# Full and half-width expert passes run side by side in a mixture-of-experts layer, and the last scatter moves ahead of a branch

## The chip, the cores and the metric

One core of one Trainium2 chip runs the whole program. The metric is device time in microseconds (us) of one execution. The kernel before has a median of 1798.19 us over 3 runs, from 1795.90 to 1801.63 us. Everything is float32 in memory.

## What is computed

Two layers of a transformer block on 256 latent and 256 context tokens of width 1024. Only the end of it matters here: in the second layer the feed-forward part is a mixture of 8 experts, and each of the 256 latent tokens goes to its two best.

```python
def swiglu(h, w1, w3, w2):
    return (jax.nn.silu(h @ w1) * (h @ w3)) @ w2

def moe_ffn(h, router, w1, w3, w2):
    ...
    logits = (ht @ router).astype(jnp.float32)
    top_v, top_i = lax.top_k(logits, TOP_K)
    wts = jax.nn.softmax(top_v, axis=-1)
    ...
    def expert_step(acc, p):
        e1, e3, e2, cw = p
        return acc + cw[:, None] * swiglu(ht, e1, e3, e2), None
```

w1 and w3 are 1024 x 2816, w2 is 2816 x 1024. After it come a norm, a gate and the residual sum. One expert's weights are 33 units of 1 MB: 22 for w1 and w3 ("up"), 11 for w2 ("down").

## The kernel before, in words

**Passes.** Each expert is one pass p. The expert order is found on the chip from the token counts: pass 0 is fixed, then the experts follow from the fullest to the emptiest. A pass collects ("gathers") the tokens of its expert into slots by matmuls with a selection matrix (`gather`, then `turn_selection`, which transposes that matrix for later), runs 11 chunks (FC = 11, numbered c) of 256 columns of the inner width, and puts the results back to their tokens by matmuls with the turned selection (`scatter`, four pieces), which VectorE adds to `y_moe` (`added`). Passes 0 to 4 have 128 slots; pass 1 has 32 more in a side computation (WIDE, its tiles end in `_wide`); passes 5, 6 and 7 have 64 slots ("narrow", `NARROW = range(5, 8)`). After these eight come up to three further passes for experts with more tokens than slots, each behind a branch on a number computed on the chip (`extra`); in the profiled execution none is taken.

**Full passes.** A product of float32 operands is made of three matmuls of rounded parts. So each 1 MB weight unit is split: ScalarE writes the rounded high part (`high`, L1360) and VectorE the rest (`low`, L2018), into a ring of `W_RING` = 4 places. The raw units arrive by DMA in a ring of `RAW_RING` = 5 places; a raw place is free for the next load once its unit is split. `unit_ready` on TensorE waits for the split.

**Narrow passes.** They take the raw unit as it is, in one float32 product on 64 columns of the array, so there is no split, but a raw place is free only when TensorE has used it.

**The steps.** `run_steps` gives, for step i, what TensorE does in a row: the up matmuls of chunk i (`up_chunk`, two units), the transposes of chunk i-1's activations (`turn_chunk`, into PSUM bank 2), the down matmuls of chunk i-2 (`down_chunk`, one unit); behind it, at certain chunks, a scatter piece of the pass before (chunks 3 to 6) or the gather for the next (chunk 7). Between them ScalarE makes silu (`silu`, L1434), VectorE the product (`product`, L2067), ScalarE copies the turned columns (`columns_turned`, L1445, for narrow chunks L1442) and VectorE makes their low part (L2078). The order on each engine is the order of the code in that engine's `run`; every engine waits on semaphores and works strictly in its own order.

**Where the splits stand.** In `run` on ScalarE and VectorE the place of each split is fixed by `split_behind`: at the step that uses split unit s, the unit s + 4 is split. So the splits run up to a ring ahead of their use. `output` copies a finished pass from PSUM for its scatter; `half_high`/`half_low` and `columns_high`/`columns_low` copy the gathered tokens from PSUM.

**The end.** On TensorE the last pass's four scatters (`finish`) stand in the Else part of the branch on further passes.

Of the kernel before, what the change touches and what calls it, by code (L numbers as in the profile page):

```python
# [32 lines left out]
P = 128  # L33
# [259 lines left out]
EXTRA = (2 * LAT - 1) // (P + 1)  # L293
PASSES_OF = EXPERTS + EXTRA
# [4 lines left out]
def run_steps(passes):  # L299

    g0, g1 = passes[0] * FC, (passes[-1] + 1) * FC
    for g in range(g0, g1 + 2):
        yield g if g < g1 else None, g - 1 if g0 <= g - 1 < g1 else None, g - 2 if g0 <= g - 2 else None


def pass_units():

    out = []
    for passes in RUNS:
        for up, _, down in run_steps(passes):  # L310
            out += [("up", up, 0), ("up", up, 1)] if up is not None else []
            out += [("down", down)] if down is not None else []
    assert len(out) == PASSES_OF * EXPERT_UNITS
    return out
# [3 lines left out]
UNIT_AT = {key: m for m, key in enumerate(UNIT_LIST)}  # L318
RUN_END = tuple((passes[-1] + 1) * EXPERT_UNITS for passes in RUNS)


def run_last(r):
    return (RUNS[r][-1] + 1) * FC - 1
# [12 lines left out]
NARROW, SLOTS = range(5, EXPERTS), 64  # L336
HALF_GROUPS = P // SLOTS


def is_narrow(p):  # L340

    return p in NARROW
# [10 lines left out]


SPLIT_LIST = [m for m, key in enumerate(UNIT_LIST) if not is_narrow(unit_of_expert(key)[0])]
SPLIT_OF = {m: s for s, m in enumerate(SPLIT_LIST)}

# [6 lines left out]
def split_limit(r):  # L364

    return split_end(r) + (0 if is_narrow(RUNS[r][-1]) else W_RING - 1)


def split_behind(r, key):

    s = SPLIT_OF[UNIT_AT[key]] + W_RING
    return [s] if s < split_limit(r) else []
# [192 lines left out]
TURN_BANK, SCATTER_BANK = 2, 3  # L565
# [3 lines left out]
def build(nc, ctx, units, x_in, ctx_in, const_in, cols_in, wsm_in, gw2_in, lam_in, rope_in, out):  # L569
# [85 lines left out]
    picked = at("picked", A_GL + 2952, [P, 2, 3, EXPERTS])  # L655
    order, order_parts = at("order", A_AM + 320, [P, EXPERTS, EXPERTS]), at("order_parts", A_GL + 3888, [P, 3, EXPERTS, EXPERTS])
    xt_plain = at("xt_plain", A_ACTT, [P, 2, KT, P])
    selT_plain = at("selT_plain", A_GL + 1280, [P, 2, 2, P])
    eT_plain = at("eT_plain", A_GL + 1792, [P, 2, 256])
    ey_plain = at("ey_plain", A_OD, [P, 512])  # L660
# [133 lines left out]
    def down_bank(p, h):  # L794

        return 4 + 2 * (p % 2) + h

    def up_bank(g):

        return 0 if g // FC == WIDE else (g + WIDE * FC) % 2  # L800

    def gather_bank(p, n):

        return SCATTER_BANK if p == WIDE + 1 else down_bank(p, n)
# [5 lines left out]
    def select_place(p):  # L810
        return sel if p < EXPERTS else sel_more[p - EXPERTS]
# [101 lines left out]
    def _(pool):  # L913
# [18 lines left out]
        def select_narrow(p):  # L932

            twice = const[:, C_IOTA:C_IOTA + SLOTS].unsqueeze(1).to_broadcast([P, HALF_GROUPS, SLOTS])
            for tt in range(2):
                pool.tensor_scalar(sel[:, tt, :].rearrange("p (j n) -> p j n", j=HALF_GROUPS), twice, route[:, tt, 4, p:p + 1],
                                   route[:, tt, 3, p:p + 1], ALU.is_equal, ALU.mult).then_inc(esem("sel"), 1)
# [11 lines left out]
        for p in range(1, EXPERTS):  # L949

            pool.wait_ge(esem("selT"), p)
# [15 lines left out]
    def _(act):  # L967
# [399 lines left out]
        def half_high(p, n):  # L1367
            act.wait_ge(esem("gathered"), 2 * p + n + 1)
            if is_narrow(p):
                act.activation(xt_plain[:, p % 2, 4 * n:4 * n + 4, 0:SLOTS],  # L1370
                               psum[:, gather_bank(p, n), 0:4 * SLOTS].rearrange("p (k n) -> p k n", n=SLOTS),
                               ACT.Copy).then_inc(esem("xt_hi"), 1)
                return
            act.activation(xt_hi[:, p % 2, 4 * n:4 * n + 4, :],
                           psum[:, gather_bank(p, n), :].rearrange("p (k n) -> p k n", n=P),
                           ACT.Copy).then_inc(esem("xt_hi"), 1)

        def selection_turned(p):
            act.wait_ge(esem("selT"), p + 1)
            if p >= 2:  # L1380
# [1717 lines left out]
```

## Time and profile before

| | before |
|---|---|
| median of 3 runs | 1798.19 us |
| profiled execution, time | 1800.37 us |
| profiled execution, span | 1798.4 us |
| TensorE busy | 1694.8 us (94%) |
| VectorE busy | 1015.4 us (56%) |
| ScalarE busy | 794.1 us (44%) |
| mean granted TensorE clock | 0.973 of full speed |
| moved by DMA | 407.53 MB, mean 227 GB/s |

The expert layer is the second half: pass 0 begins near 973 us after the span's start, pass 2 near 1217 us, the narrow passes near 1520 us, and the last down matmul ends near 1778 us. In the rows below times are us from the span's start. PE is TensorE, DVE VectorE, ACT ScalarE, POOL GpSimd, SP SyncE. "[2.0 <-X]" says that the engine sat idle for 2.0 us and that X ended it. Matmuls overlap, so the distance of two starts is what one costs, and its own length is longer. PEclk is the granted TensorE clock as a share of 2.4 GHz.

### The profile page before, as it was taken

To read this page: it belongs to the slowest core of one execution; us is meant where nothing else is said; L and a number is where in the kernel's file an instruction comes from. 1 tells how busy PE (TensorE), PEld (TensorE's weight loads), DVE (VectorE), ACT (ScalarE), POOL (GpSimd) and SP (SyncE) were. 2 spreads that over 40 slices of the span, in tenths; PEclk is the share of its full clock that TensorE was granted. 3 is DMA by queue.
4 is the path that set the end of the run, shared out by engine and by line. 5 is a ranking of instruction groups with operands and counts; after the bars stand their busy time and mean duration, and the time that the engine had idled before them with its cause. 6 is when DMAs were issued, how large, how long until landed. Compare 5 with 4: busy or idle time off the path is not lost.

```text
span 1798.4 us, 25945 instructions
## 1 busy us (share of the span) xinstructions
PE 1694.8 (94%) x10337; PEld 1310.9 (73%) x10337; DVE 1015.4 (56%) x1403; ACT 794.1 (44%) x1225; POOL 55.0 (3%) x40
## 2 busy tenths in 40 slices
PE   6999989999999999999887999999999998889886
PEld 4877668988888888887677887777788887444442
DVE  3335656677677434643766986667799895101012
ACT  4416545622212223725546765556677774100101
POOL 0000000000000000000000530000000000000000
PEclk8999989999999999999978999999999999999998
DMA  8412053244467422231024977668999897899997
GB/s 332 150 71 71 1 201 145 79 185 170 185 237 263 179 94 94 80 117 48 24 71 151 357 287 258 237 235 354 344 351 360 343 360 295 327 421 421 420 421 327
DMA packets 56830, 407.53 MB, mean 227 GB/s; under 512 B 6322, under 2 KB 6450, under 8 KB 7808
## 3 DMA queue, kind: packets, MB, share of 16 engines
q1 hardware_dynamic: 56128, 404.38, 58.6%
q8 instruction: 85, 1.39, 0.3%
q0 software_dynamic: 288, 0.79, 0.1%
q10 hardware_dynamic: 288, 0.63, 0.1%
q14 instruction: 41, 0.34, 0.1%
HBM read 404.73 MB, written 1.05 MB: 226 GB/s over the span
## 4 chain that ended last, share of the span: by engine, by line
PE 82%; DMA 7%; DVE 5%; ACT 4%; issue 2%; SPq 0%; POOL 0%; DVEq 0%; ACTq 0%
PE psum L2243 60%; PE psum L2850 4%; DMA raw_more<-units 4%; DMA raw<-units 4%; PE psum L2860 2%; PE psum L2748 2%; PE psum L2806 1%; PE psum L2876 1%; PE psum L2888 1%; PE psum L2442 1%; PE psum L2269 1%; DVE w_lo L1551 1%; PE psum L2466 1%; PE psum L2538 1%; PE psum L2260 1%
## 5 line engine op out<-in xcount | busy, mean ns | idle before, releaser
L1551 DVE TENSOR_TENSOR w_lo<-raw,w_hi 128x1024 fp32r<-128x1024 f32 x130 | 153.0, 1220 | 144.9 <-ACT w_hi L980 144.6
L2243 PE MATMUL psum<-act_hi,w_hi 128*128 128x512 f32 (+1 forms) x608 | 221.1, 364 | 2.1 <-DVE w_lo L1551 2.1
L2243 PE MATMUL psum<-act_hi,w_lo 128*128 128x512 f32 (+1 forms) x608 | 218.7, 360 | 0.0
L2243 PE MATMUL psum<-act_lo,w_hi 128*128 128x512 f32 (+1 forms) x608 | 218.7, 360 | 0.0
L980 ACT ACTIVATE w_hi<-raw 128x1024 fp32r<-128x1024 f32 x130 | 130.3, 1053 | 161.8 <-DMA raw<-units 87.5
L2018 DVE TENSOR_TENSOR w_lo<-raw,w_hi 128x2048 fp32r<-128x2048 f32 x75 | 171.5, 2289 | 41.7 <-ACT w_hi L1360 41.4
L1360 ACT ACTIVATE w_hi<-raw 128x2048 fp32r<-128x2048 f32 x75 | 143.8, 1918 | 68.4 <-PE psum L2243 43.2
L2018 DVE TENSOR_TENSOR w_lo<-raw_more,w_hi 128x2048 fp32r<-128x2048 f32 x49 | 112.1, 2289 | 46.2 <-ACT w_hi L1360 46.0
L2243 PE MATMUL psum<-w_hi,act_hi 128*128 128x256 f32 (+1 forms) x368 | 130.2, 354 | 3.4 <-DVE w_lo L1551 1.7
L2243 PE MATMUL psum<-w_hi,xt_hi 128*128 128x512 f32 x332 | 132.1, 398 | 0.0
L2243 PE MATMUL psum<-w_lo,xt_hi 128*128 128x512 f32 x332 | 129.9, 391 | 0.0
L2243 PE MATMUL psum<-w_hi,xt_lo 128*128 128x512 f32 x332 | 129.7, 391 | 0.0
L2067 DVE TENSOR_TENSOR e_act<-e_sil,psum 128x256 f32<-128x256 f32 (+1 forms) x88 | 32.2, 366 | 172.4 <-ACT e_sil L1434 172.4
L2243 PEld LDWEIGHTS psum<-act_hi,w_hi 128*128 128x128 f32 x608 | 115.5, 190 | 19.1 <-DVE w_lo L1551 2.7
L2243 PEld LDWEIGHTS psum<-act_hi,w_lo 128*128 128x128 f32 x608 | 115.3, 190 | 17.6
L2243 PEld LDWEIGHTS psum<-act_lo,w_hi 128*128 128x128 f32 x608 | 115.4, 190 | 16.5
L2243 PE MATMUL psum<-w_lo,act_hi 128*128 128x256 f32 (+1 forms) x368 | 123.1, 334 | 0.0
L2243 PE MATMUL psum<-w_hi,act_lo 128*128 128x256 f32 (+1 forms) x368 | 123.0, 334 | 0.0
L1360 ACT ACTIVATE w_hi<-raw_more 128x2048 fp32r<-128x2048 f32 x49 | 94.0, 1918 | 65.7 <-DMA raw_more<-units 35.0
L1434 ACT ACTIVATE e_sil<-psum 128x256 f32<-128x256 f32 (+1 forms) x88 | 29.4, 334 | 197.5 <-PE psum L2850 193.4
L1608 DVE SCALAR_TENSOR_TENSOR folded<-raw,c_cols,folded 128x512 f32<-128x512 f32 x140 | 101.5, 750 | 3.3
L2243 PEld LDWEIGHTS psum<-w_hi,act_hi 128*128 128x128 f32 x368 | 69.8, 190 | 26.0 <-issue 12.0
(363 smaller groups left out, 3249.3 us busy)
## 6 DMA issues: line engine op xcount, KB each, us to landing
raw<-units SPq DMA_DIRECT2D x275, 1024.0 KB, 5.1
raw_more<-units SPq DMA_DIRECT2D x107, 1024.0 KB, 6.7
X<-ctx_in SPq DMA_DIRECT2D x1, 1024.0 KB, 8.5
X<-x_in SPq DMA_DIRECT2D x1, 1024.0 KB, 10.6
out<-X SPq DMA_DIRECT2D x2, 512.0 KB, 2.8
const<-const_in ACTq DMA_DIRECT2D x1, 524.0 KB, 7.4
rope<-rope_in POOLq DMA_DIRECT2D x2, 256.0 KB, 4.9
wsm<-wsm_in SPq DMA_DIRECT2D x1, 384.0 KB, 7.0
```

The costliest lines, as they stand in the source:

```text
L980: act.activation(w_hi[:, w_slot(i), part], raw[:, i % RING, part], ACT.Copy).then_inc(hi_ready, 1)
L1360: act.activation(w_place(m)[0], raw_place(m), ACT.Copy).then_inc(esem("w_high"), 1)
L1434: act.activation(e_sil[:, g % 2, 0:n], psum[:, up_bank(g), 0:n], ACT.Silu).then_inc(esem("sil"), 1)
L1551: ins = dve.tensor_tensor(w_lo[:, w_slot(i), part], raw[:, i % RING, part], w_hi[:, w_slot(i), part].bitcast(F32), ALU.subtract)
L1608: ins = dve.scalar_tensor_tensor(total, part, share, total, ALU.mult, ALU.add)
L2018: dve.tensor_tensor(lo, raw_place(m), hi.bitcast(F32), ALU.subtract).then_inc(esem("w_ready"), 1)
L2067: dve.tensor_tensor(e_act[:, g % 2, 0:n], e_sil[:, g % 2, 0:n], psum[:, up_bank(g), n:2 * n], ALU.mult).then_inc(esem("act"), 1)
L2243: ins = pe.matmul(dst, lhs(a), rhs(b), start=first and n == 0, stop=last and n == 2)
L2260: ins = pe.matmul(bank(key)[group, 0:256], c_cols[:, k, :], raw[:, n % RING, k * 256:(k + 1) * 256], start=k < 4, stop=k >= 4)
L2748: ins = pe.matmul(psum[:, gather_bank(p, n), (k % 4) * slots:(k % 4 + 1) * slots], src[:, tt, k * P:(k + 1) * P], select_place(p)[:, tt, 0 ...
L2850: ins = pe.matmul(psum[SLOTS * j:SLOTS * (j + 1), up_bank(g), 0:2 * P].rearrange("p (g n) -> p g n", g=2), xt_plain[:, p % 2, k, 0:SLOTS], ...
L2860: ins = pe.matmul(psum[SLOTS * h:SLOTS * (h + 1), down_bank(p, 0), :], eT_plain[:, g % 2, SLOTS * j:SLOTS * (j + 1)], weight[:, j * D_MODE ...
```

## The change

Three things change in the code.

1. The narrow passes become 3, 5 and 7, each beside the full pass ahead of it: the pairs are 2 and 3, 4 and 5, 6 and 7. The ranks are handed out so that the same three emptiest experts stay narrow (`PLACE_OF_RANK`). In a pair one step holds both: up of the full chunk, up of the narrow one, turn of the full one and of the narrow one, down of both. A step thus takes six units, 6 MB.
2. In the pairs the full chunks have PSUM bank 0 for up and banks 4 and 5 for down, the narrow ones banks 1 and 6; both kinds turn into bank 2. Tiles of the narrow passes get places of their own. Every split of a pair is written in the step that uses it (`splits_at` gives `[s]`), where before it was s + 4. The gather for the next pair is cut into pieces that stand at chunks 7, 8, 9 and 10; the scatters stand at chunks 2 to 5 (full pass, or pass 1) and 6 to 9 (narrow pass); the outputs stand at chunk 2, ahead of the splits of that step.
3. On TensorE `finish` stands ahead of the branch. Since two passes (6 and 7) are then still to be put back, it has eight scatters and not four. On ScalarE the outputs of the last passes move into the branch.

The diff, cut to its core. The order of passes, steps, splits and gather pieces:

```diff
+PLACE_OF_RANK = (0, 1, 2, 5, 3, 6, 4, 7)
...
-NARROW, SLOTS = range(5, EXPERTS), 64
+NARROW, SLOTS = (3, 5, 7), 64
+FIRST_PAIR = 2
...
+def run_steps(r):
+
+    rows = []
+    for p in RUNS[r]:
+        if not is_narrow(p):
+            beside = (p + 1,) if is_narrow(p + 1) else ()
+            rows += [tuple(q * FC + c for q in (p,) + beside) for c in range(FC)]
+    for i in range(len(rows) + 2):
+        yield tuple(rows[j] if 0 <= j < len(rows) else () for j in (i, i - 1, i - 2))
...
-def split_behind(r, key):
-
-    s = SPLIT_OF[UNIT_AT[key]] + W_RING
-    return [s] if s < split_limit(r) else []
+def splits_at(r, key):
+
+    s = SPLIT_OF[UNIT_AT[key]]
+    if r == 0 and s >= SINGLE_SPLITS:
+        return [s]
+    return [s + W_RING] if s + W_RING < (split_limit(r) if r else SINGLE_SPLITS) else []
...
+def gather_pieces(r, p, c):
+
+    if r or p == 0 or is_narrow(p) or not 0 <= c - GATHER_STEP < 4:
+        return []
+    a = p + 1 if p == WIDE else p + 2
+    pieces = [[(a, 0)], [(a, 1)], [(a, 2), (a + 1, 0)], [(a + 1, 1), (a + 1, 2)]][c - GATHER_STEP]
+    return [piece for piece in pieces if piece[0] <= EXPERTS]
```

ScalarE's `run`, as it is now (VectorE's has the same order, with `low`, `product` and `half_low`):

```diff
+            for ups, turned, downs in run_steps(r):
+                full = [g for g in ups if not is_narrow(g // FC)]
+                for g in full:
+                    p, c = divmod(g, FC)
...
+                    if p >= FIRST_PAIR:
+                        for q in outputs_at(r, p, c):
+                            output(q)
+                    for s in splits_at(r, ("up", g, 0)):
+                        high(s)
...
+                    for s in splits_at(r, ("up", g, 1)):
+                        high(s)
+                    if p != WIDE:
+                        silu(g)
+                if len(ups) == 2:
+                    for g in downs[:1]:
+                        for s in splits_at(r, ("down", g)):
                             high(s)
+                    silu(ups[1])
+                for g in turned:
+                    columns_turned(g)
...
+                for g in full:
+                    p, c = divmod(g, FC)
+                    for q, piece in gather_pieces(r, p, c):
+                        half_high(q, piece) if piece < 2 else selection_turned(q)
```

TensorE's turn and end:

```diff
         def turn_chunk(g):
 
-            pe.wait_ge(esem("act"), g + 1)
-            if g:
-                wait_turned_columns(g - 1)
+            pe.wait_ge(esem("act"), CHUNK_AT[g] + 1)
+            for h in CHUNKS[max(CHUNK_AT[g] - 2, 0):CHUNK_AT[g]]:
+                wait_turned_columns(h)
...
         def finish(p):
-            for n in range(4):
-                scatter(p, n, n)
+            for q in last_passes(0) if p < EXPERTS else (p,):
+                for n in range(4):
+                    scatter(q, n, n)
 
         def extra(k):
+            finish(RUNS[k][-1])
             with pe.If(run_valid(pe, k)):
...
-            with pe.Else():
-                finish(EXPERTS + k - 1)
```

How the change moves instructions shows at three places.

ScalarE in a full pass before, around the gather for the next pass at chunk 7. `w_hi` is the high part of a weight unit, `xt_hi` the gathered tokens, `e_sil` silu, `eT_hi` the turned columns, `more_arrived` the semaphores of the raw ring.

```order
L1434 ACTIVATE e_sil<-psum 128x256 [waits e_act,e_w_used]
L1445 ACTIVATE eT_hi<-psum 128x256 [waits e_w_used,e_turned]
L1360 ACTIVATE w_hi_more<-raw 128x2048 [waits more_arrived1,e_w_used]
L1374 ACTIVATE xt_hi<-psum 128x512 [waits e_gathered] x2
L1383 ACTIVATE selT<-psum 128x256 [waits e_scattered,e_selT]
L1360 ACTIVATE w_hi<-raw 128x2048 [waits more_arrived2,e_w_used]
L1360 ACTIVATE w_hi<-raw_more_149 128x2048 [waits more_arrived3,e_w_used]
```

The same place now, in a pair, at chunk 7 and up to the next silu.

```order
L1560 ACTIVATE eT_hi<-psum 128x256 [waits e_w_used,e_turned]
L1558 ACTIVATE eT_plain<-psum 128x128 [waits e_w_used,e_turned]
L1488 ACTIVATE xt_hi<-psum 128x512 [waits e_gathered]
L1473 ACTIVATE w_hi<-raw 128x2048 [waits more_arrived0,e_w_used]
L1473 ACTIVATE w_hi<-raw 128x2048 [waits more_arrived1,e_w_used]
L1550 ACTIVATE e_sil<-psum 128x256 [waits e_act,e_w_used]
```

Both have a copy of gathered tokens ahead of two splits. Before, those splits are of units used a ring later; now the first `w_hi` behind the copy is that of the unit with which TensorE's next step begins.

TensorE in a pair now, from the end of a narrow up chunk to the begin of the next step's up (the 11 rows of the down matmuls between are left out by "...").

```order
L3016 MATMUL psum<-raw_more_153,xt_plain 64x256 x7
L3057 MATMUL psum<-const,e_act 128x128 [waits e_eT_hi,e_eT_lo,e_act]
L3057 MATMUL psum<-const,e_act 128x128
L3054 MATMUL psum<-const,e_act_plain 128x128 [waits e_eT_lo,e_eT_hi,e_act]
L2394 MATMUL psum<-w_hi,eT_hi 128x512 [waits e_w_ready,e_ey_lo,e_eT_lo]
...
L3026 MATMUL psum<-raw,eT_plain 64x512 [waits more_arrived0,e_ey_hi,e_eT_hi]
L3026 MATMUL psum<-raw,eT_plain 64x512 x3
L2970 MATMUL psum<-ey_hi,selT 128x512 [waits e_added,e_selT_copy,e_ey_lo]
L2970 MATMUL psum<-ey_lo,selT 128x512
L2394 MATMUL psum<-w_hi,xt_hi 128x512 [waits e_w_ready,e_act]
```

Before, one turn stood in each step, and it waited for the copies of the step before. Now the narrow turn (L3054) waits for `e_eT_lo`, the low part of the full chunk that was turned in the row ahead of it.

## Rows read from the trace of the kernel before

**Rows 1.** Busy time by stretch: from:to, length, busy us (count) per engine, PEclk, DMA share, GB/s
```profile
1303.25:1336.95 33.70, 33.70 (x154) 27.73 (x152) 30.18 (x21) 25.21 (x20) 0.00 (x0) 1.00 0.88 339
...
1597.93:1634.67 36.74, 30.39 (x207) 15.29 (x206) 1.44 (x5) 3.30 (x12) 0.00 (x0) 1.00 1.01 421
1212.09:1777.90 565.81, 534.30 (x2943) 365.96 (x2939) 283.32 (x241) 239.09 (x267) 7.22 (x8) 0.99 0.93 369
1777.90:1798.40 20.50, 5.79 (x8) 1.79 (x8) 8.24 (x14) 5.50 (x14) 0.00 (x0) 0.59 0.56 229
```

**Rows 2.** Timeline of TensorE in the full passes: start, length, line, matmuls
```profile
1212.09 0.44 PE L2888 MATMUL psum<-const,e_act 128*128 128x128 f32 x2
...
1216.66 0.50 PE L2243 MATMUL psum<-w_hi,xt_hi 128*128 128x512 f32 x1
...
1253.46 1.12 PE L2806 MATMUL psum<-ey_wide,selT_wide 64*128 64x512 f32 x2
...
1303.25 0.38 PE L2888 MATMUL psum<-const,e_act 128*128 128x128 f32 x2
```

**Rows 3.** Timeline of TensorE in the narrow passes
```profile
1592.35 0.33 PE L2888 MATMUL psum<-const,e_act 128*128 128x128 f32 x1
1592.61 1.94 PE L2860 MATMUL psum<-raw_more,eT_plain 128*64 128x512 f32 x8
1594.38 3.62 PE L2850 MATMUL psum<-raw,xt_plain 128*64 128x256 f32 x32
1597.93 0.33 PE L2888 MATMUL psum<-const,e_act 128*128 128x128 f32 x1
...
1652.12 1.12 PE L2806 MATMUL psum<-ey_plain,selT_plain 64*128 64x512 f32 x2
```

**Rows 4.** Groups by form, ScalarE and VectorE, 1212 to 1778 us: busy us, mean ns
```profile
L1360 ACT ACTIVATE w_hi<-raw 128x2048 fp32r<-128x2048 f32 x44 | 84.4, 1919 | 35.9 <-PE psum L2243 33.0 <-DMA raw<-units 2.8
L1445 ACT ACTIVATE eT_hi<-psum 128x256 fp32r<-128x256 f32 x35 | 13.2, 378 | 3.1 <-PE psum L2888 3.1
L1434 ACT ACTIVATE e_sil<-psum 128x128 f32<-128x128 f32 x33 | 9.2, 278 | 193.4 <-PE psum L2850 193.4
L1374 ACT ACTIVATE xt_hi<-psum 128x512 fp32r<-128x512 f32 x6 | 3.6, 592 | 7.4 <-PE psum L2748 7.4
L1370 ACT ACTIVATE xt_plain<-psum 128x256 f32<-128x256 f32 x6 | 2.3, 381 | 12.0 <-PE psum L2748 12.0
L2018 DVE TENSOR_TENSOR w_lo<-raw,w_hi 128x2048 fp32r<-128x2048 f32 x45 | 103.0, 2288 | 18.9 <-ACT w_hi L1360 18.6
L2078 DVE TENSOR_TENSOR eT_lo<-psum,eT_hi 128x256 fp32r<-128x256 f32 x35 | 14.6, 417 | 1.1 <-ACT eT_hi L1445 1.1
L2067 DVE TENSOR_TENSOR e_act<-e_sil,psum 128x128 f32<-128x128 f32 x33 | 9.5, 287 | 172.4 <-ACT e_sil L1434 172.4
```

**Rows 5.** The chain that ended last, in order of time, 1500 us to the end
```profile
1521.73 4.69 DMA raw_more<-units
...
1584.86 3.69 PE psum L2748 x32
```

**Rows 6.** Busy time by stretch, around idle spells of TensorE: columns as in rows 1
```profile
954.50:959.10 4.60, 0.00 (x0) 0.00 (x0) 2.48 (x6) 4.16 (x12) 0.00 (x0) 0.97 0.00 0
959.10:965.70 6.60, 5.70 (x32) 4.34 (x33) 3.30 (x6) 3.28 (x8) 0.00 (x0) 0.50 0.43 159
...
1531.50:1535.70 4.20, 4.15 (x11) 3.42 (x12) 0.52 (x2) 0.38 (x1) 0.00 (x0) 0.50 0.00 0
...
1556.00:1564.00 8.00, 6.58 (x49) 3.21 (x47) 1.08 (x3) 0.53 (x2) 0.00 (x0) 1.00 1.01 423
```

**Rows 7.** Timeline of TensorE and ScalarE: idle spells inside and at the end of the narrow passes
```profile
1531.55 0.66 PE L2888 MATMUL psum<-const,e_act 128*128 128x128 f32 x2 [8.28 <-DVE eT_lo L2078]
...
1783.12 3.75 PE L2806 MATMUL psum<-ey_plain,selT_plain 64*128 64x512 f32 x6 [5.24 <-issue]
1784.04 1.28 ACT L1501 ACT_TABLE_LOAD   x1 [5.39 <-issue]
```

More of the change, by code:

```diff
@@ L296, with is_narrow @@
 RAW_RING, W_RING = 5, 4
[L299 to L303, printed above, removed]
+NARROW, SLOTS = (3, 5, 7), 64
+FIRST_PAIR = 2
+def is_narrow(p):
+    return p in NARROW
+def run_steps(r):
[6 more added lines that the diff above has]
+        yield tuple(rows[j] if 0 <= j < len(rows) else () for j in (i, i - 1, i - 2))
+CHUNKS = [g for r in range(len(RUNS)) for ups, _, _ in run_steps(r) for g in ups]
+CHUNK_AT = {g: n for n, g in enumerate(CHUNKS)}
 def pass_units():
     out = []
[L309 to L312, printed above, removed]
+    for r in range(len(RUNS)):
+        for ups, _, downs in run_steps(r):
+            out += [("up", g, i) for g in ups for i in range(2)]
+            out += [("down", g) for g in downs]
     assert len(out) == PASSES_OF * EXPERT_UNITS
@@ new lines, in run @@
+                    if p != WIDE:
+                        silu(g)
+                if len(ups) == 2:
+                    for g in downs[:1]:
+                        for s in splits_at(r, ("down", g)):
+                            high(s)
+                    silu(ups[1])
+                for g in turned:
+                    columns_turned(g)
+                if len(ups) < 2:
+                    for g in downs[:1]:
+                        for s in splits_at(r, ("down", g)):
+                            high(s)
@@ L1511, in extra @@
             with act.If(run_valid(act, k)):
+                for q in last_passes(k):
+                    output(q)
                 for s in range(split_limit(k), split_end(k) + W_RING):
@@ L2123, in _ @@
+            for q in last_passes(r):
+                output(q)
         descending_once = const[:, C_DESC:C_DESC + EXPERTS]
@@ L2933, in run @@
         def run(r):
[L2934 to L2947 removed]
+            for ups, turned, downs in run_steps(r):
+                for g in ups:
+                    up_chunk(g)
+                for g in turned:
+                    turn_chunk(g)
+                for g in downs:
+                    down_chunk(g)
+                for g in ups[:1]:
+                    p, c = divmod(g, FC)
+                    for q, n in scatters_at(r, p, c):
+                        scatter(q, n)
+                    for q, piece in gather_pieces(r, p, c):
+                        gather_piece(q, piece)
+                    if c == GATHER_STEP and (p == 0 or r and p + 1 < PASSES_OF):
                         gather(p + 1)
```

390 lines of the change are left out of this document (229 added, 161 removed).

## The prediction

> **What bounds the kernel now.** I read the busy shares by stretch first. In a full pass TensorE is busy for all of the 33.70 us of four chunks, 8.43 us a chunk, with the DMA engines at 0.88 [rows 1]. In a narrow pass DMA is at 1.01 and TensorE is busy for 30.39 of 36.74 us [rows 1] and 421 GB/s, so a unit of 1.05 MB takes 2.49 us and a chunk's three take 7.47. So full passes are bound by TensorE and narrow ones by DMA, and laying one beside the other looks like a gain: a pair's step needs six units, 14.9 us, of DMA, and TensorE needs 8.43 for the full chunk and 5.58 for a narrow one whose data is there (from turn to turn, [rows 3]), 14.0 us. Now the two take 8.43 + 7.47 = 15.9 us one after the other. The stretch that the change rewrites, from the turn at 1212.09 (pass 1, chunk 9) to the end of the last down matmul at 1777.9, is 565.8 us, of which TensorE works 534.3 [rows 1]. It holds one large wait, 8.28 us at 1531.55 [rows 7], where the kinds of pass change.
>
> Next I read what feeds TensorE. A split is 1.92 us on ScalarE and then 2.29 us on VectorE [rows 4]; before it is hidden, since splits run four units ahead. The change gives this up in the pairs: each split stands in the step that uses it, behind everything that ScalarE did in the step before.
>
> **An ordinary step of a pair**, by the chain of waits, t = 0 at TensorE's first full up matmul. The matmuls of a full chunk are 36 in 8.43 - 0.2 us [rows 1, 2], 0.228 each: up 24, to 5.5, done 5.65. ScalarE then makes silu (0.4) and splits the down unit, 6.05 to 8.0; VectorE's low part ends at 10.3. Meanwhile the narrow up, 3.6 us [rows 3], has ended at 9.1 to 9.2; its product on VectorE (0.29) waits behind the low part, to 10.55; the low part of the turned full columns (0.42) follows, to 10.95 [rows 4]. Only then may TensorE turn the narrow chunk, from 11.0 to 11.3: 1.5 us idle behind the full turn. Now two paths run to the next step: TensorE's down matmuls, 12 x 0.23 and 1.8 for the narrow one [rows 3], to 15.8; and ScalarE's copy of the narrow turn (0.28), the split's high part (1.92), VectorE's low part (2.29), with semaphores to 15.9. **Step: 15.9 us**, not 14.9, and with no reserve between the two paths. Transfers are in time: the down unit is asked for at the end of the step before and is wanted 6.0 us later; a transfer took 4.69 us [rows 5].
>
> **The sum of the stretch.**
> - 33 steps x 15.9, less 1.0 for the first, which has no narrow turn: 523.7.
> - Scatters at the end of a step: four with the wide part, 1.6 each (1.12 and two matmuls, [rows 2]), eight full at 0.45, eight narrow at 1.1 [rows 3], less 0.1 of reserve: 17.
> - Gathers of passes 4, 6 and 8, 3.7 each as now [rows 5], and of 5 and 7, the same, with the turned selections: 19.5.
> - **Waits for a split behind a gather piece.** ScalarE reaches its copy of the gathered tokens and waits there until TensorE has ended downs, scatter and piece. Then copy 0.6, high 1.92, low 2.29, with semaphores 4.9 us [rows 4], in which TensorE has nothing to do, since the next up unit isn't split. Narrow pieces have two copies of 0.38, 5.1 us. Pieces stand at chunks 7 to 10 of pairs 1 and 2, at 7 to 9 of pair 3: 6 x 4.9 + 4 x 5.1 + 4.7 = 54.5. One more at pass 1's chunk 10, as the first pair's units are no longer split ahead: 5.1.
> - **Waits for a split behind the outputs** at chunk 2: the copy of the pass that has just ended (0.7) comes ahead of the split, 5.1 us, and 6.0 in the first pair, where `ey_wide` and both halves come first: 16.2.
> - From the turn at 1212.09 to the first pair: 4.6 as now [rows 2], and 2.0 of gather. At the end two steps with downs alone, the first again behind its split: 15.1.
>
> Together 523.7 + 17 + 19.5 + 54.5 + 5.1 + 16.2 + 6.6 + 15.1 = 657.7, against 565.8: **+92**. The wait of 8.28 us that goes is inside this difference. Ahead of the stretch, the narrow pass's first piece at pass 1's chunk 9 adds 1.9, and eight memsets in a row on VectorE in pass 0 add 2 (not shown; nothing if TensorE never waits there, 4 if each costs a round through its semaphore; the middle, since VectorE has under 1 us of reserve per chunk): +4.
>
> **The clock.** There are then 15 waits of about 5 us. Around an idle 4.60 us the granted clock fell to 0.50 for the 6.60 us behind it, and behind the 8.28 us it was 0.50 for another 4.2 [rows 6, 7]. The work done at half speed cost half of those stretches, 3.3 and 2.1 us. In the stretch with narrow waits of up to 1.4 us it stayed at 1.00 [rows 6], so I charge nothing for the 1.5 us inside each ordinary step. I take 2.5 us a wait, between those two and nearer to the second, since that one lies in expert passes as these will: 15 x 2.5 = +37. Bounds: nothing (the clock holds) and 3.3.
>
> The Trainium skill, TensorE: Matmul & The Clock Gate, section on HAM oscillation, tells of a kernel in which each tile's wait for data threw the engine back to the lower clock, so that every tile paid anew. By that rule all 15 waits pay, as summed here. No row yet shows a wait of 5 us with dense matmuls on both sides; if the clock holds there, the sum is 37 us less (rival 2).
>
> **The end.** Now 5.24 us pass between ScalarE's last copies and TensorE's scatter, ended by no other engine [rows 7], and 20.5 us between the last matmul and the end [rows 1]. With the scatters ahead of its branch TensorE doesn't wait there itself, but VectorE's branch still stands between its last output and its adds, and there are eight adds of 0.75 us in place of four. What leaves, about 4, is taken by the four further adds, 3: -1, with -5 (all branches hidden) and +3 (none) as bounds.
>
> **Sum:** +92 + 4 + 37 - 1 = +132 on the profiled 1800.4, 1932. The median of the runs is 2.2 below the profiled time, so I forecast **1930 us**.
>
> **Rivals.**
> 1. *The splits are hidden and the pairs overlap as they are meant to*: faster. Then a step costs the larger of 14.9 and TensorE's work: 14.9 for chunks 0 to 6, 16 to 17 where a gather piece stands, near 170 us a pair, 510 in all, with 17 at both ends 527, so 39 less; with +4 and -1 that is 1800.4 - 36 - 2 = 1762. For it speaks DMA's 1.01 beside an unsaturated TensorE [rows 1]. Against it is the order: ScalarE's `w_hi` for the next step stands behind a copy that waits for that step's end. It decides where TensorE waits under 0.3 us at a step's begin; the halfway point is waits of some 2 us. 7 in 100.
> 2. *The waits are as summed, but the clock holds at full speed*: 1930 - 37 = 1893. The gaps stand 16 to 20 us apart with dense work between, unlike the one at 954 us. 13 in 100.
> 3. *More than summed*: the clock costs 3.3 us a wait (+12), or the down unit comes late, since two narrow units are on their way ahead of it; each us over its 6.0 adds one to the 18 ordinary steps, so 1 to 2.4 us late is +18 to +43. 1942 to 1985, about 1965. 17 in 100.
> 4. *It does nothing that can be measured*, waits and gains cancel: 2 in 100. It would need waits of 1.5 us where I find 5.
>
> The forecast's own case has 61 in 100, from 1905 to 1950. **Range** 1885 to 1975: it takes in rival 2 and most of rival 3, and leaves out rival 1. A measurement of this kernel tells about 0.3% (5 us) from no change. Faster 0.07, same 0.02, slower 0.91.
>
> **What would show it.** The timeline of ScalarE at chunks 7 to 10 of a pair: `xt_hi` or `xt_plain` released by a gather matmul, `w_hi` right behind it, `w_lo` on VectorE, and TensorE's next matmul released by `w_lo` after 4.9 to 5.1 us; 12 such waits, and 3 behind `ey_plain` or `ey_hi`. Ordinary steps of 15.9 us with the narrow turn released by `eT_lo` after some 1.5 us. The granted clock at 0.50 behind each long wait. DMA busy near 0.75 over the stretch, from 0.93, so that it is the bound no longer. TensorE waits for no transfer. I am wrong if steps with a gather piece are under 20 us (expected 22 to 24), if ordinary ones are near 15 or over 17, or if TensorE's waits name a DMA.

## The result, and the profile after

The change takes **1938.82 us** (median of 4 runs, 1933.78 to 1941.59), the kernel before 1799.91 in the same comparison (4 runs, 1795.9 to 1807.18): ratio 1.0755, 95% interval 1.0718 to 1.0793. The forecast was 1930 us, range 1885 to 1975. The profiled execution of the change took 1933.78 us. Each ratio below is to the kernel before in the same comparison; its median moved from 1798.5 to 1804.8 us between comparisons, so times from different ones compare to some 5 us.

The page of the changed kernel: the span, the busy times, the granted clock, and the chain that ended last.

```profile
span 1931.9 us, 25970 instructions
...
PE 1737.2 (90%) x10337; PEld 1325.1 (69%) x10337; DVE 1018.0 (53%) x1416; ACT 792.0 (41%) x1225; POOL 51.7 (3%) x40
...
PEclk8999899999999999997989999999888998899988
...
PE 71%; DVE 12%; ACT 8%; issue 7%; DMA 1%; SPq 0%; POOL 0%; DVEq 0%; ACTq 0%
```

The last row is the chain. VectorE and ScalarE hold 20% of it, and DMA 1%: what is waited for is computed, not loaded. The digits of PEclk are 8 in seven of the last fourteen slices, those of the pairs.

Busy time by stretch, columns as in [rows 1]: the rewritten stretch from the turn of pass 1, chunk 9 to the end of the last down matmul, the tail, an ordinary step (turn to turn), a step with a full scatter (up to up), a step with a gather piece, and a long wait with what follows it.

```profile
1212.25:1913.65 701.40, 576.34 (x2920) 378.37 (x2916) 285.01 (x237) 242.03 (x270) 4.69 (x6) 0.92 0.79 301
1913.65:1931.90 18.25, 6.14 (x18) 2.99 (x16) 10.79 (x18) 4.02 (x12) 0.00 (x0) 0.67 0.41 166
...
1459.51:1475.44 15.93, 14.68 (x81) 9.63 (x80) 7.74 (x7) 6.72 (x7) 0.00 (x0) 1.00 0.98 391
1509.67:1526.66 16.99, 15.47 (x81) 9.92 (x82) 8.48 (x7) 6.72 (x7) 0.00 (x0) 1.00 0.96 369
1386.27:1410.43 24.16, 18.01 (x95) 12.54 (x96) 8.43 (x7) 7.31 (x8) 0.00 (x0) 0.86 0.66 260
...
1368.75:1373.65 4.90, 0.00 (x1) 0.03 (x1) 3.13 (x3) 4.19 (x3) 0.00 (x0) 0.67 0.64 241
1373.65:1378.00 4.35, 4.35 (x12) 3.44 (x13) 2.06 (x1) 0.00 (x0) 0.00 (x0) 0.59 0.73 266
```

Against [rows 1] the stretch is 135.6 us longer (701.4 for 565.8) and the tail 2.2 shorter (18.3 for 20.5). Of the 135.6, busy TensorE time is 42 us (576.3 for 534.3), most of it the same matmuls at the lower clock, and the rest is idle time. The DMA share fell from 0.93 to 0.79.

TensorE's waits over 1190 to 1960 us: total, times, longest.

```profile
PE psum L2394 <- DVE w_lo L2144: 63.2, 22, 5.9
PE psum L3054 <- DVE eT_lo L2207: 41.0, 33, 1.3
PE psum L2394 <- DVE w_lo_more L2144: 20.7, 8, 5.0
PE psum L2970 <- DVE y_moe L2184: 2.8, 1, 2.8
```

No transfer is among them. The first and third row hold 15 waits of 4.7 to 5.9 us at the begin of a step, one more of 4.6 in the drain, and small ones. One of the 15, on all engines (start, length, engine, line; in brackets the idle time and what ended it):

```profile
1593.96 0.28 PE L2899 MATMUL psum<-sel,h_lo 128*128 128x128 f32 x1
1594.27 0.60 ACT L1488 ACTIVATE xt_hi<-psum 128x512 fp32r<-128x512 f32 x1 [7.41 <-PE psum L2899]
1594.76 3.70 ACT L1473 ACTIVATE w_hi<-raw 128x2048 fp32r<-128x2048 f32 x2
1594.90 0.69 DVE L2154 TENSOR_TENSOR xt_lo<-psum,xt_hi 128x512 fp32r<-128x512 f32 x1 [8.80 <-ACT xt_hi L1488]
1596.70 2.29 DVE L2144 TENSOR_TENSOR w_lo<-raw,w_hi 128x2048 fp32r<-128x2048 f32 x1 [1.11 <-ACT w_hi L1473]
...
1599.13 0.76 PE L2394 MATMUL psum<-w_hi,xt_hi 128*128 128x512 f32 x1 [4.90 <-DVE w_lo L2144]
```

ScalarE was idle for 7.41 us though the raw unit was there (over 1190 to 1960 us it waits for one only twice, 2.6 us in all): it stood at the copy of the gathered tokens, which could only begin when TensorE had ended its step. Only then came the split for TensorE's next matmul. The wait is copy, high part, low part, in a row, and TensorE works in none of it.

### The profile page after: what moved, and what is told of

The parts are those of the page before. It is cut to its first block, busy times and chain, and to the rows that moved or that the text cites. A ratio compares the mean times of both kernels' runs of the same rounds, so it can differ in the third digit from the quotient of the medians.

```text
span 1931.9 us, 25970 instructions
## 1 busy us (share of the span) xinstructions
PE 1737.2 (90%) x10337; PEld 1325.1 (69%) x10337; DVE 1018.0 (53%) x1416; ACT 792.0 (41%) x1225; POOL 51.7 (3%) x40
## 3 DMA queue, kind: packets, MB, share of 16 engines
HBM read 404.73 MB, written 1.05 MB: 210 GB/s over the span
## 4 chain that ended last, share of the span: by engine, by line
PE 71%; DVE 12%; ACT 8%; issue 7%; DMA 1%; SPq 0%; POOL 0%; DVEq 0%; ACTq 0%
PE psum L2394 53%; DVE w_lo L2144 4%; ACT w_hi L1473 4%; PE psum L3026 3%; PE psum L2899 2%; DVE w_lo_more L2144 1%; PE psum L2970 1%; DMA raw<-units 1%; ACT w_hi_more L1473 1%; PE psum L3042 1%; PE psum L2593 1%; PE psum L2420 1%; DVE w_lo L1677 1%; PE psum L2617 1%; PE psum L2689 1%
## 5 line engine op out<-in xcount | busy, mean ns | idle before, releaser
L2394 PE MATMUL psum<-w_hi,xt_hi 128*128 128x512 f32 x332 | 146.5, 441 | 63.5 <-DVE w_lo L2144 63.4
L2394 PE MATMUL psum<-w_lo,xt_hi 128*128 128x512 f32 x332 | 140.9, 424 | 0.0
L2394 PE MATMUL psum<-w_hi,xt_lo 128*128 128x512 f32 x332 | 138.6, 418 | 0.0
L1550 ACT ACTIVATE e_sil<-psum 128x256 f32<-128x256 f32 x55 | 20.9, 379 | 274.9 <-PE psum L2394 274.9
L2394 PEld LDWEIGHTS psum<-w_hi,xt_hi 128*128 128x128 f32 x332 | 69.4, 209 | 91.7 <-issue 69.1
L2394 PEld LDWEIGHTS psum<-act_lo,w_hi 128*128 128x128 f32 x608 | 115.6, 190 | 16.5
L2196 DVE TENSOR_TENSOR e_act<-e_sil,psum 128x256 f32<-128x256 f32 x55 | 23.0, 418 | 163.8 <-ACT e_sil L1550 163.8
```

The lines of the kernel that those rows point to most:

```text
L1550: act.activation(e_sil[:, parity(g), :], psum[:, up_bank(g), 0:256], ACT.Silu).then_inc(esem("sil"), 1)
L2196: dve.tensor_tensor(e_act[:, parity(g), :], e_sil[:, parity(g), :], psum[:, up_bank(g), 256:512], ALU.mult).then_inc(esem("act"), 1)
L2394: ins = pe.matmul(dst, lhs(a), rhs(b), start=first and n == 0, stop=last and n == 2)
```

## The experiments

**1 to 4: each suspected cost alone.** e1_splits_ahead, in `run` on ScalarE (on VectorE the same with `low`); `ahead_of` gives the up units of the next step if that is a pair's:

```diff
+                for key in ahead_of(r, i):
+                    for s in splits_at(r, key):
+                        high(s)
                 for g in full:
                     p, c = divmod(g, FC)
                     for q, piece in gather_pieces(r, p, c):
```

(and the two `splits_at(r, ("up", g, k))` of a pair's own step are gone).

> ACT and DVE split both up units of the next pair step right after the turned copies, ahead of the gather copies and the outputs; TensorE's order is that of the change. Theory A (the 15 waits of 4.7 to 5.9 us end with DVE's split only because it stands behind the gather copies or outputs on ACT and DVE): the waits go (15 x 5.0 = 75 us), with them the time at half clock behind them (34 us in the trace of the change) and some 0.7 us in each of 12 scatter steps (8 us); 1939 - 117 = about 1822 us, granted clock of the stretch back to 0.97 or more. Theory B (the stretch is held by transfers, and the splits only end a wait that a transfer would end as late): the waits on DVE are replaced by waits on DMA at the same places, and the time falls by under 40 us, to 1900 or more.

Measured: **1835.66 us**, ratio to before 1.0199 (1.0143 to 1.0254); 103 us less than the change. Its waits of TensorE:

```profile
PE psum L3067 <- DVE eT_lo L2217: 48.7, 33, 3.0
PE psum L2407 <- DVE w_lo_more L2154: 5.0, 2, 4.6
...
PE psum L2407 <- DVE w_lo L2154: 1.2, 2, 0.8
```

The waits for `w_lo` fell from 83.9 to 6.2 us; the 4.6 left is the drain's. Theory A stands: TensorE waits for no transfer in their place, and ScalarE's waits for raw units are 19.3 us in all. The missing 14 us against 1822: the narrow turn now waits up to 3.0 us in steps that hold a copy or an output too (48.7 for 41.0), with the clock at 0.66 to 0.72 for 5 us behind the three of 2.8 us and more and at 1.00 behind the next one down, 2.45 us, and the profiled stretch is 597.9 us, 103.5 less and not 117:

```profile
1212.10:1810.00 597.90, 542.96 (x2920) 359.04 (x2916) 284.53 (x237) 243.96 (x270) 5.25 (x6) 0.99 0.91 353
```

The clock, 0.92 in this stretch of the change, is 0.99 again.

e2_full_first changes TensorE's `run` alone, in steps with two up chunks:

```diff
-                for g in turned:
+                for g in turned[:1] if len(ups) == 2 else turned:
                     turn_chunk(g)
-                for g in downs:
+                for g in downs[:1] if len(ups) == 2 else downs:
+                    down_chunk(g)
+                for g in turned[1:] if len(ups) == 2 else ():
+                    turn_chunk(g)
+                for g in downs[1:] if len(ups) == 2 else ():
                     down_chunk(g)
```

> TensorE alone has another order: turn full, down full, turn narrow, down narrow, so that the narrow turn's silu has a down chunk of time to end. The narrow turn waits 1.25 us for eT_lo in each of 33 steps of the change. Theory A (in such a step the splits of ACT and DVE, which stand behind the narrow turned copies, come due next): the 1.25 us is gained, but the narrow turn is later by the full down chunk (3.6 us), the turned copies and splits behind it are later by as much, and the next up units wait; about 2 us more an ordinary step and 1 a scatter step: 1939 + 15 to 50 = 1955 to 1990 us. Theory B (the wait for the silu is just time lost): 33 x 1.25 = 41 us less, 1898 us.

Measured: **1963.77 us**, 1.0910 (1.0851 to 1.0969). Theory A. The 41 us at the narrow turn went, and the waits for `w_lo` rose from 83.9 to 135.9 us:

```profile
PE psum L2394 <- DVE w_lo L2144: 103.5, 50, 6.0
PE psum L2394 <- DVE w_lo_more L2144: 32.4, 17, 5.0
...
PE psum L3054 <- DVE eT_lo L2207: 1.0, 1, 1.0
```

In its timeline one sees why. ScalarE waits 3.44 us for the narrow turn before it may split:

```profile
1553.09 0.28 ACT L1558 ACTIVATE eT_plain<-psum 128x128 f32<-128x128 f32 x1 [3.44 <-PE psum L3054]
1553.26 3.70 ACT L1473 ACTIVATE w_hi<-raw_more 128x2048 fp32r<-128x2048 f32 x2
...
1555.19 2.29 DVE L2144 TENSOR_TENSOR w_lo<-raw_more,w_hi 128x2048 fp32r<-128x2048 f32 x1 [4.86 <-ACT w_hi L1473]
...
1557.63 0.47 PE L2394 MATMUL psum<-w_hi,xt_hi 128*128 128x512 f32 x1 [2.06 <-DVE w_lo L2144]
```

e5_keep_busy gives TensorE work in the gaps:

```diff
+        def keep_busy(g):
+            pe.wait_ge(esem("act"), CHUNK_AT[g] + 1)
+            for _ in range(20):
+                pe.matmul(psum[:, WIDE_UP_BANK, :], h2_hi[:, 0, 0:P], h2_hi[:, 0, 0:512], start=True, stop=True)
...
+                    if r == 0 and p >= FIRST_PAIR and (c == 1 or gather_pieces(r, p, c)):
+                        keep_busy(g + FC)
```

> The kernel of the change with 20 added matmuls of 128x512, whose results are not used, in 15 places where TensorE waits 4.7 to 5.9 us for w_lo; the waits stay, but TensorE has work in them (20 x 0.228 = 4.6 us). Theory A (the waits cost a second time, because the clock falls to its lower level after each): the granted clock stays at 1.0 behind them and 15 x 2.3 = 34 us go, less what the added matmuls stick out by (15 x 0.3): about 1908 us. Theory B (the clock fell for another cause, as load or a fixed interval): the lower clock stays and the time is 1939 to 1950 us.

Measured: **1914.08 us**, 1.0630 (1.0583 to 1.0677), 24.7 less than the change though it computes more. (The edit reached 14 of the 15 gaps; pass 1's last chunk kept its 5.02.) The same kind of step as 1386.27 to 1410.43 above, in this kernel:

```profile
1391.58:1414.31 22.73, 21.17 (x116) 15.08 (x116) 8.43 (x7) 7.33 (x8) 0.00 (x0) 1.00 0.76 277
...
1380.66 0.47 PE L2394 MATMUL psum<-w_hi,xt_hi 128*128 128x512 f32 x1 [0.31 <-DVE w_lo L2144]
```

Clock 1.00 for 0.86, the step 1.4 us shorter, a first matmul of 0.47 us in place of 0.77. So these falls of the clock follow from the idle gap and are paid on top of it. The Trainium skill says as much (TensorE: Matmul & The Clock Gate, section on HAM oscillation: each tile's wait sends the engine back to the lower clock); here it holds for the 15 gaps of 4.7 us and more and for e1's three of 2.8 to 3.0 us, while the clock stayed at 1.00 in steps with a gap of 1.25 us.

e4_scatter_behind_branch undoes the second part of the change: `finish(RUNS[k][-1])` goes back behind the branch, into both arms.

> The last scatter stands again behind the branch on further passes, in both of its arms; all else is the change. Theory A: TensorE's branch (5.2 us of issue before the change) comes back on the path between the last down chunk and the scatter, where 1.9 us passes now: the tail after the last down grows by 3 to 4.5 us, 1939 to about 1942.5 us. Theory B (the branch is hidden under the wait for DVE's own branch of 4.5 us): no change in the tail, within 0.5 us.

Measured: 1943.65 us, 1.0802 (1.0756 to 1.0848), 4.8 more. That looks like theory A, and isn't. The tail of e4 from the end of its last down matmul, and rows of the change's tail (18.25 us, above):

```profile
1918.28:1937.20 18.92, 5.59 (x17) 3.33 (x16) 10.97 (x18) 3.95 (x12) 0.00 (x0) 0.75 0.40 160
...
1921.39 0.76 PE L2970 MATMUL psum<-ey_hi,selT 128*128 128x512 f32 x1 [3.11 <-issue]
```
```profile
1917.70 4.04 DVE L2184 SCALAR_TENSOR_TENSOR y_moe<-psum,route,y_moe 128x512 f32<-128x512 f32 x6 [4.50 <-issue]
1918.59 4.02 PE L2970 MATMUL psum<-ey_plain,selT_plain 64*128 64x512 f32 x8 [2.82 <-DVE y_moe L2184]
```

TensorE's branch shows (3.11 us of issue), but the tail is only 0.7 us longer, because in the change TensorE runs ahead into VectorE's branch (4.50) and waits 2.82 there. The rest has nothing to do with the edit. In the two profiled executions the stretch is 698.7 us in e4 and 701.4 in the change, though its code is the same, and its first turn stands at 1219.6 us and at 1212.25.

Nearly all of that shift of the first turn lies further ahead, in front of pass 0, where no experiment edits the kernel. The first turn of pass 0 stands anywhere from 987.5 to 996.9 us over the fourteen traces. From it to the turn of pass 1, chunk 9, three executions with the code of before take 219.5 to 219.6 us, and eleven with the change's code 224.6 to 224.8 (first row before, second the change):

```profile
992.49:1212.09 219.60, 219.60 (x1664) 167.69 (x1662) 164.45 (x170) 132.46 (x130) 42.35 (x20) 1.00 0.75 274
```
```profile
987.58:1212.25 224.67, 223.05 (x1679) 170.68 (x1677) 162.82 (x182) 129.18 (x129) 41.61 (x22) 0.99 0.74 266
```

So terms are read inside a trace, between two marks in the code, and medians of kernels a few us apart aren't enough.

**5 to 7: what is left when the splits are ahead.** e3_ahead_and_full_first is e1 and e2 together (TensorE's order now in the last steps too), with ScalarE's narrow copy behind the splits ahead:

```diff
-                for g in turned:
+                for g in turned[:1]:
                     columns_turned(g)
                 for key in ahead_of(r, i):
                     for s in splits_at(r, key):
                         high(s)
+                for g in turned[1:]:
+                    columns_turned(g)
```

> Both orders at once: ACT and DVE split the next pair step's up units ahead (as in e1_splits_ahead), TensorE runs turn full, down full, turn narrow, down narrow (as in e2_full_first), and ACT copies the narrow turned columns behind the splits. Alone the first gave 1836 us and the second 1964 us. Theory A (the second order lost only because the splits stood behind the narrow turned copies): now the 33 narrow turns wait for nothing, 48.7 us in the trace of e1_splits_ahead, and the time is 1836 - 45 = about 1790 us, under the 1799 of before. Theory B (transfers limit: the step of 15.93 us moved 391 GB/s x 15.93 us = 6.2 MB with a DMA share of 1.00 already): the gain comes only in the 26 steps that have a scatter or gather in them, 26 x 1.25 = 33 us, and new waits for DMA stand in the 7 others: 1800 to 1805 us. Theory C (the orders don't add): 1836 us or more.

Measured: **1820.78 us**, 1.0082 (1.0053 to 1.0111). e2's order, which cost 25 us alone, gains 15 here (21 by the ratios), so A's mechanism is there, but A's and B's times were both missed. A step of the first pair with a scatter went only from 17.4 us in e1 to 16.8 to 17.0, and a new wait stands in each of the 33: the down matmuls wait 0.72 us or more for their split. ScalarE, in its turn, waits for raw units 74.7 us in all:

```profile
ACT w_hi L1480 <- DMA raw<-units: 33.7, 27, 2.8
...
ACT w_hi L1480 <- DMA raw_more<-units: 16.3, 14, 2.3
...
ACT w_hi_more L1480 <- DMA raw<-units: 13.8, 9, 3.3
...
ACT w_hi_more L1480 <- DMA raw_more<-units: 10.9, 8, 2.6
```

e6_and_drain_ahead splits the two last down units a step earlier too (`ahead_of` returns `("down", steps[i + 1][2][0])` where the next step has no ups).

> e3_ahead_and_full_first, and ACT and DVE split the two last down units one step earlier, ahead of the turned copies. The last down step waits 4.58 us for w_lo_more in every trace of the change, with some 2 us at half clock behind it. Theory A (the split is late by its place in the order): 6.6 us less than e3_ahead_and_full_first. Theory B (the raw unit arrives late, so the split can't be earlier): the same within 1 us, the wait on DMA.

Measured: 1816.55 us, 1.0072 (1.0040 to 1.0103), 4.2 less than e3; the intervals overlap, so the median doesn't settle it. In the trace the drain's wait of 4.6 to 4.7 us is gone and its last turns stand 5.1 us apart, 11.5 in e3; from the first turn of pass 0 to the end e6 takes 821.6 us and e3 828.8. That is theory A.

e7_added_behind is the change with `added` of the pairs moved behind `low` of the second up unit on VectorE.

> The kernel of the change, in which DVE adds a scatter's result to y_moe behind the split of the second up unit and not ahead of it. The pair steps with a full scatter last 17.0 us where 15.9 + 0.35 (eight more matmuls, less what they hide) was reckoned, and TensorE waits 0.28 us for w_lo in them. Theory A (added stands on DVE between the two splits and waits for the scatter to end, so the second split is late): 0.3 to 0.7 us less in each of 12 scatter steps, 1939 - 4 to 8 = 1931 to 1935 us. Theory B (the 17.0 us are TensorE's own work): unchanged within 1 us, 1939 us.

Measured: 1937.01 us, 1.0741 (1.0710 to 1.0772): 1.8 less than the change, less than theory A's 4 to 8 and within the scatter of starts. The steps with a full scatter are 16.4 us for 17.0 and TensorE's 0.28 us wait is gone from all but one, so A holds for the step; but narrow turns behind them wait up to 1.8 to 2.5 us, and over the whole stretch nothing is seen to be gained: 698.2 us, where e4 and e13 below, with `added` in its old place, have 698.7 and 698.3. Before the edit, on VectorE of the change:

```profile
1503.41 2.29 DVE L2144 TENSOR_TENSOR w_lo<-raw,w_hi 128x2048 fp32r<-128x2048 f32 x1 [2.60 <-ACT w_hi L1473]
1506.66 0.75 DVE L2184 SCALAR_TENSOR_TENSOR y_moe<-psum,route,y_moe 128x512 f32<-128x512 f32 x1 [0.96 <-PE psum L2970]
1507.33 2.28 DVE L2144 TENSOR_TENSOR w_lo_more<-raw,w_hi_more 128x2048 fp32r<-128x2048 f32 x1
...
1509.67 0.50 PE L2394 MATMUL psum<-w_hi_more,xt_hi 128*128 128x512 f32 x1 [0.28 <-DVE w_lo_more L2144]
```

**8 to 12: is a transfer the floor?** e8_down_split_early adds to e6, on ScalarE (VectorE likewise), the down split ahead of the full silu:

```diff
                     for s in splits_at(r, ("up", g, 1)) if r or p < FIRST_PAIR else []:
                         high(s)
+                    for s in splits_at(r, ("down", downs[0])) if len(ups) == 2 and downs else []:
+                        high(s)
                     if p != WIDE:
                         silu(g)
```

> e6_and_drain_ahead, and in the pair steps ACT and DVE split the full down unit right behind the second up unit, ahead of the full chunk's silu and product (in e3_ahead_and_full_first and e6_and_drain_ahead ACT waits some 7 to 8 us for the up matmuls before that silu, and the down matmuls wait 0.72 us or more for w_lo in each of 33 steps, 38 us in all). Theory A (the down split is late by its place): 33 x 0.72 = 24 us or more go, 1816 - 24 = about 1792 us, under the 1799 to 1804 of before. Theory B (transfers hold the stretch: in e3 the splits waited 75 us for raw units): the waits for w_lo turn into waits for DMA and the time stays above 1808 us.

Measured: **1811.60 us** (12 runs), 1.0035 (1.0016 to 1.0054) against 1804.78 of before (23 runs). Theory B. TensorE's waits for `w_lo` are 32.1 us, and ScalarE's for raw units rose from 74.7 in e3 and 85.0 in e6 to 232.8:

```profile
PE psum L2409 <- DVE w_lo L2157: 25.6, 29, 2.3
...
ACT w_hi L1482 <- DMA raw<-units: 99.9, 37, 7.3
ACT w_hi L1482 <- DMA raw_more<-units: 75.5, 28, 7.6
...
1286.36:1319.84 33.48, 32.26 (x168) 20.61 (x166) 16.80 (x15) 13.68 (x14) 0.00 (x0) 1.00 0.97 381
```

The last row is two steps, 16.74 us each: 381 GB/s x 16.74 us = 6.4 MB, which is the six units of a pair's step (6 x 1.05 = 6.3). A step lasts as long as its weights take. From the first turn of pass 0 to the end e8 takes 816.8 us and the kernel before 805.9, so e8 is still 11 us behind it; 5.1 of them lie ahead of the stretch (e4, above).

e11_half_narrow_loads is e8 with half of each narrow unit's columns loaded; e13_change_half_loads and e12_before_half_loads are the same edit in the change and in the kernel before:

```diff
-            sp.dma_start(raw_place(m), units[bass.ds(at_expert(p) * EXPERT_UNITS + (first - EXPERT_UNITS + place), 1)].rearrange(
-                "a p n -> (a p) n")).then_inc(more_arrived[m % RAW_RING], 16)
+            n = UNIT // 2 if is_narrow(p) and m < RUN_END[0] else UNIT
+            sp.dma_start(raw_place(m)[:, 0:n], units[bass.ds(at_expert(p) * EXPERT_UNITS + (first - EXPERT_UNITS + place), 1)].rearrange(
+                "a p n -> (a p) n")[:, 0:n]).then_inc(more_arrived[m % RAW_RING], 16)
```

> e8_down_split_early with half of each narrow pass's weight unit loaded (the other half of the place holds older numbers, so the three narrow passes compute with partly wrong weights; the instructions are the same). 99 units of 1 MB become half as large, 52 MB less of the 212 MB of the stretch. Theory B of e8 (transfers hold the stretch): 10 to 25 us less than e8_down_split_early, no waits for DMA on ACT. Theory A (TensorE's own work and the splits hold it): the same within 3 us.

> The kernel of the change with half of each narrow pass's weight unit loaded (the other half of the place holds older numbers, so the three narrow passes compute with partly wrong weights; the instructions are the same). Theory A (the change is slow by the order of the splits on ACT and DVE, no transfer is waited for): 1939 us, unchanged within 3 us, the 15 waits of 5 us as they were. Theory B (transfers have a part in the 15 waits or in the step of 15.93 us): 10 us less or more than that.

> The kernel before with the same half loads for the narrow passes (again with partly wrong weights there). Its narrow passes, 1560 to 1778 us, moved 419 GB/s with a DMA share of 1.01 and TensorE was idle for 22.4 us of 218. Theory A (there transfers set the pace, so this idle time is all that running them beside full passes could win): 12 to 22 us less, 1780 to 1790 us. Theory B (TensorE and its copies set the pace there too): within 5 us of before, and nothing was to be won by the pairing.

Measured: e11 **1778.40** (0.9851, 0.9827 to 0.9875), 33.2 less than e8 and more than the 10 to 25 expected; e13 **1935.11** (1.0719, 1.0654 to 1.0784), 3.7 less than the change; e12 **1775.09** (0.9820, 0.9758 to 0.9882), 26.4 less than the 1801.45 of before, again more than the 12 to 22 expected. In e13 TensorE waits as in the change:

```profile
PE psum L2395 <- DVE w_lo L2145: 63.2, 22, 5.9
PE psum L3055 <- DVE eT_lo L2208: 41.0, 33, 1.2
PE psum L2395 <- DVE w_lo_more L2145: 20.7, 8, 5.0
```

So the 15 waits have nothing to do with transfers: with a quarter fewer bytes in the stretch they add up to the same tenth. The median fell by 3.7 us where theory A allowed 3, but the intervals of the ratios overlap, and the profiled stretch is 698.3 us, as long as e4's 698.7 with every byte loaded. In the kernel before they do set the pace of the narrow passes. The first row is before, the second e12, where TensorE has no idle time left:

```profile
1560.00:1778.00 218.00, 195.55 (x1297) 98.67 (x1297) 17.69 (x41) 19.96 (x71) 1.57 (x2) 1.00 1.01 419
```
```profile
1555.00:1753.00 198.00, 198.00 (x1365) 103.12 (x1363) 19.00 (x44) 20.99 (x74) 1.57 (x2) 0.98 0.74 243
```

That bounds what any pairing could win from the wait for transfers: about 26 us. It isn't all that a pairing can win, since the wait of 8.28 us where full passes give way to narrow ones [rows 7] stands in e12 too (8.31 us), with slow matmuls behind it, and a pairing has no such place: by 8.3 us and the 2.1 that the prediction took for them an estimate of 10 us more. And e11, the best order found with a quarter fewer bytes to load, only comes near what e12 reaches without pairs. e11 expected no DMA waits on ScalarE; there are still 163.8 us of them, which hold TensorE for 9 us in all.

e10_before_scatter_ahead is the kernel before with the second part of the change alone:

```diff
         def extra(k):
+            finish(EXPERTS + k - 1)
             with pe.If(run_valid(pe, k)):
...
-            with pe.Else():
-                finish(EXPERTS + k - 1)
```

> The kernel before, with only the last scatter moved ahead of the branch on TensorE, as the change has it. Theory A (TensorE's branch, 5.2 us of issue between the last down chunk and the scatter, is on the path that sets the end): 3 to 5 us less, 1795 to 1798 us. Theory B (ACT's and DVE's own branches, of like length, hold the end in its place): within 1 us of before.

Measured: 1800.03 us (12 runs), 0.9985 (0.9966 to 1.0003) against 1804.78: 2.7 us less by the ratio, and the interval just takes in 1. In the trace, from the end of the last down matmul (1776.8) to the end:

```profile
1776.80:1794.20 17.40, 3.10 (x9) 1.04 (x8) 8.06 (x14) 5.24 (x14) 0.00 (x0) 0.71 0.68 277
```

17.4 us for 20.5 [rows 1] and for the 19.4 of e12, whose end has the code of before: 2 to 3 us less. TensorE's branch was on the path in the kernel before (theory A) and hardly in the change, where VectorE's has taken its place. The gain shows in the tail and isn't proved for the whole: in the same trace the stretch ahead of it, whose code is that of before, happened to be 568.6 us for 565.8.

No version that loads all the weights is shown to be faster than the kernel before. A sixth place for raw units, which might let transfers run on through the gather steps, wasn't tried.

## Why the prediction was right

The mechanism, its places and its sign were right, and the time to within half a per cent: forecast 1930, measured 1938.8. That the time is so near is in part luck, since the same stretch took 698 to 701 us in different executions and what lies ahead of pass 0 varies by 9. Term by term, on the profiled execution:

- **Ordinary step**, 15.9 summed: 15.93. The idle time before the narrow turn is 1.25 us, 1.5 was summed.
- **Waits behind a gather piece, pass 1's last chunk and the outputs**, 54.5 + 5.1 + 16.2 = 75.8: the 15 waits are 75.1 (eleven of 4.7 to 5.0 behind pieces; 5.0; 5.9, 5.0 and 5.1 behind outputs). e1 takes them away by order alone and e13 shows that no transfer has a part in them. This is the term that decides, and the chain through one copy and one split gave it to 1%.
- **Scatters**, 17 summed: too low. A step with a full scatter takes 17.0 us, not 16.25, one with a narrow 17.4, not 16.9, one with the wide 18.0, not 17.4; together some 10 us (six of the eight narrow ones stand in a step with a gather piece and cost the 1.0 summed). The step that failed is "less 0.1 of reserve": a scatter was charged its matmuls on TensorE, and what stands on VectorE behind it was left out. `added` waits for the scatter's end and stands between the two splits that TensorE needs next (e7: 16.4 us without it there).
- **The clock**, 15 x 2.5 = 37: the matmuls behind the 15 waits lost 1.5 to 3.1 us each, 34.2 in all, and 2.1 behind the drain's. e5 shows it causal: the stretch is 26 us shorter (675.3 for 701.4), of the 32.7 lost behind the 14 gaps that it fills; the rest comes back in steps that are a little longer. Rival 2 (the clock holds) falls.
- **The stretch** in all: 657.7 + 37 = 694.7 summed, 701.4 measured. What isn't scatters and ordinary steps was summed 2 to 3 us too high, so two errors offset each other in part.
- **Ahead of the stretch**, +4 (1.9 for the gather piece and 2 for the eight memsets, which no row showed): +5.1, from the first turn of pass 0 to the turn of pass 1, chunk 9. The gather piece is 1.75 of it (14.42 us from turn to turn for 12.67). The memsets take 0.94 us together and lie ahead of the wait below, by which that step is 1.0 us longer. The other 2.3 us weren't foreseen: a wait of 0.64 us for `w_lo` at 1034.6, and 1.6 us in the step with pass 1's side gather. There the clock falls with no idle gap ahead, behind 3.5 us of matmuls of only 32 columns; in the kernel before it stays at 1.00 behind the same matmuls. Why it differs isn't shown. The wait of 0.99 us, and the 3.5 us behind the side gather, at 0.52:

```profile
994.43 0.41 PE L3057 MATMUL psum<-const,e_act 128*128 128x128 f32 x2 [0.99 <-DVE eT_lo L2207]
...
1056.40:1059.90 3.50, 3.50 (x10) 2.77 (x10) 1.60 (x1) 0.39 (x1) 3.50 (x3) 0.52 0.98 393
```

- **The end**, -1: -2.2. ScalarE's branch, 5.39 us in the kernel before [rows 7], shows 0.40 us of issue in the change while TensorE still has its last down chunks to do; VectorE's stays, 4.50.
- **Sum**: 135.6 + 5.1 - 2.2 = 138.5, less the 4.9 us by which pass 0 happened to begin earlier, is 133.5, the difference between the two profiled spans. The medians differ by 138.9.

Rival 1 (the pairs overlap as meant, 1762 us) was priced too well even as a rival. e1, e3, e6 and e8 are that case, made step by step: 1836, 1821, 1817, 1812. It took a pair's step at 14.9 us by the 421 GB/s of a narrow pass alone [rows 1]; the pairs got 381 and needed 16.7. Rival 3's late down unit didn't happen: the change is too slow to be short of weights.

## What to carry to other kernels

When two kinds of work are interleaved to balance two resources, walk the producing engines' order first: what prepares the next step must stand ahead of every instruction that waits for the present one, and an idle gap of TensorE costs its length and the slow matmuls behind it, here 5.0 + 2.3 us. Before such a change, halve the suspected resource's load in the kernel as it is (e12): one such kernel gives the ceiling of what hiding that resource can win, here 26 us of 1800.

## What the chip showed that was not expected

- **Transfers are slower in the pairs.** At a DMA share of 0.97 to 1.01 the narrow passes of before get 419 to 421 GB/s, steps of the pairs in the change, e1 and e8 get 381 to 392. The Trainium skill (Perfetto Trace Analysis, section Roofline) puts a lone core's ceiling at about 435 GB/s; the narrow passes come near, the pairs don't. By 381 the floor of a pair's step is 16.5 us, not 14.9. ScalarE and VectorE read and write whole weight units meanwhile, but that alone doesn't explain it: in e1, with ScalarE busy for 3.99 of 5 us in both, the stretch from 1535.64 us gets 367 GB/s and the one from 1451.10 gets 413. The cause is open.
- **A reordering can change sign.** TensorE's full-first order costs 25 us with late splits and gains 15 or more with early ones.
- **The engines' branches** cost 3.1 to 5.4 us of issue each where nothing hides them ([rows 7], e4, the change). With all three engines' near the end, taking one off the path uncovers the next.
- **The stages ahead of the expert layer vary by 9 us** between executions (the first turn of pass 0 at 987.5 to 996.9), as much as e8 gains on e3, while the 220 us behind that turn repeat to 0.2.
